# Values at rest and probabilities moving in the softmax attentions of a two-block kernel

## What is computed

```python
# first block, each of 2 layers
s = (q_nope . k_nope + q_rope . k_rope) * 96 ** -0.5      # "mla": 8 heads, width 96, values 64 wide
p = softmax(where(causal, s, neg));  o = p @ v
# top-128 of the index scores, gathered keys                # "dsa": 4 heads, one shared key and value head
p = softmax(where(valid, q . k_sel * scale, neg));  o = p @ v_sel
# second block, each of 2 layers                            # "nsa": selected and window branches,
p_s = masked_softmax(s_s, key_pos <= tq);  o_s = p_s @ v_sel   #  6 heads each in 2 groups, summed with gates
p_w = masked_softmax(s_w, m_w);            o_w = p_w @ v_win   #  12 heads in one stage
```

## Time and profile before

| | us |
|---|---|
| Runs of the kernel | 3297.77, 3294.56, 4249.05 (median 3297.77) |
| The profiled execution | 3300.15, of which the traced span is 3298.4 |
| TensorE busy in the span | 3144.2 |
| VectorE, ScalarE, GpSimd busy | 1812.1, 1302.5, 391.2 |
| mean granted TensorE clock | 0.984 of full speed |

### The profile page before, as it was taken

How to read it: one execution, slowest core, us unless ns; L and a number is a source line. 1 busy time by engine, 2 the same in 40 slices (tenths; PEclk the granted TensorE clock), 3 DMA queues, 4 the chain that set the end, 5 groups by cost and what they waited for, 6 DMA issues and landing times. The chain is left out here.

```text
span 3298.4 us, 48870 instructions
## 1 busy us (share of the span) xinstructions
PE 3144.2 (95%) x19216; PEld 2651.6 (80%) x19216; DVE 1812.1 (55%) x3220; ACT 1302.5 (39%) x2692; POOL 391.2 (12%) x374
## 2 busy tenths in 40 slices
PE   8999999999999999979999999999899999999996
PEld 6878788877878888868888878888788878788885
DVE  4875443425865424337566457474475565574744
ACT  4454432334354413233374333233443653332324
POOL 1031000001040000001213302010004034010100
PEclk9999999999999999989999999999999999999998
DMA  4111222212202222132100122222222000222230
GB/s 169 55 52 39 90 91 101 90 69 91 74 1 77 90 99 93 51 105 104 65 1 2 40 83 99 91 101 87 73 99 85 1 2 28 83 93 93 93 110 35
DMA packets 37342, 239.55 MB, mean 73 GB/s; under 512 B 4464, under 2 KB 5232, under 8 KB 15088
## 3 DMA queue, kind: packets, MB, share of 16 engines
q1 hardware_dynamic: 36528, 234.21, 20.1%
q10 hardware_dynamic: 576, 2.10, 0.2%
HBM read 234.19 MB, written 2.10 MB: 72 GB/s over the span
## 5 line engine op out<-in xcount | busy, mean ns | idle before, releaser
L265 PE MATMUL ps<-b_hl,bff_whl 128*128 128x512 f32 x704 | 274.1, 389 | 3.1 <-DVE b_hl L667 3.1
L267 PE MATMUL ps<-b_hl,bff_whl 128*128 128x512 f32 x704 | 273.9, 389 | 0.0
L266 PE MATMUL ps<-b_hl,bff_whl 128*128 128x512 f32 x704 | 273.9, 389 | 0.0
L248 DVE SCALAR_TENSOR_TENSOR bff_whl<-ring,b_cols,bff_whl 128x512 fp32r<-128x512 f32 (+1 forms) x224 | 153.2, 745 | 197.3 <-ACT bff_whl L235 197.1
L245 DVE TENSOR_TENSOR aff_whl<-ring,aff_whl 128x512 fp32r<-128x512 f32 x160 | 99.8, 685 | 222.8 <-ACT aff_whl L233 222.7
L235 ACT ACTIVATE bff_whl<-ring,b_cols 128x512 fp32r<-128x512 f32 (+1 forms) x224 | 136.6, 682 | 176.4 <-PE ps L267 176.4
L266 PE MATMUL ps<-aff_whl,a_u 128*128 128x512 f32 x512 | 204.3, 399 | 0.0
L265 PE MATMUL ps<-a_hl,aff_whl 128*128 128x512 f32 x512 | 199.5, 390 | 3.1 <-DVE a_hl L667 3.1
L265 PE MATMUL ps<-aff_whl,a_u 128*128 128x512 f32 x512 | 201.7, 394 | 0.0
L267 PE MATMUL ps<-aff_whl,a_u 128*128 128x512 f32 x512 | 200.7, 392 | 0.0
L267 PE MATMUL ps<-a_hl,aff_whl 128*128 128x512 f32 x512 | 199.2, 389 | 0.0
(11 more groups left out here) (524 smaller groups left out, 7746.5 us busy)
## 6 DMA issues: line engine op xcount, KB each, us to landing
ring<-in_a_w_ff SPq DMA_DIRECT2D x64, 1024.0 KB, 4.6
ring<-in_b_w_up SPq DMA_DIRECT2D x32, 1024.0 KB, 4.7
ring<-in_a_w_in SPq DMA_DIRECT2D x16, 1024.0 KB, 5.9
ring<-in_b_w_down SPq DMA_DIRECT2D x16, 1024.0 KB, 4.6
ring<-in_b_w_in_att SPq DMA_DIRECT2D x12, 1024.0 KB, 4.7
ring<-in_b_w_up SPq DMA_DIRECT2D x16, 768.0 KB, 4.0
ring<-in_b_w_in_conv SPq DMA_DIRECT2D x12, 768.0 KB, 4.2
ring<-in_a_w_out SPq DMA_DIRECT2D x8, 1024.0 KB, 4.8
```

Source lines behind the costliest of these rows:

```text
L248: self.c.nc.vector.scalar_tensor_tensor(out=self.part(j, 1, k), in0=src[:, k, :], scalar=g[:, row + k:row + k + 1], in1=self.part(j, 0, k) ...
L265: nc.tensor.matmul(bank, sh, mh, start=start, stop=False)
L266: nc.tensor.matmul(bank, sh, ml, start=False, stop=False)
L267: return nc.tensor.matmul(bank, sl, mh, start=False, stop=stop)
```

## The change

`softmax_attention` now takes pairs of heads (`AttentionPair`). For each head the product with the values is one group of four products after the head's fourth tile: for key tile j the values are the weights, 128 columns wide (the 64 of this head beside 64 zeros, on the side that its place in the pair says), and the turned probabilities of query tiles j to 3 move (512, 384, 256 and 128 columns). Both heads of a pair add into one PSUM bank (6), which then holds the pair's output turned: 128 value columns by 512 queries. VectorE copies it to `oT`, TensorE turns it back in four transposes to bank 7, and VectorE divides both heads at once. `pT` holds all four tiles of two heads. The turned probabilities of a head's last tile are copied by VectorE, those of the other three by ScalarE. The mask of mla goes to TensorE as in dsa and nsa. The zeros beside the values are written by GpSimd at the start of the stage (`place`); in nsa it also moves one group's values. In nsa heads h and h+3, of different groups, are a pair, and the queries are split in that order. Two copies that make float32r versions of the identity and the mask join mla's transposing stage on ScalarE.

```diff
+                    u = i - 4
+                    if ends(u):
+                        h = units[u][0]
+                        if h == 0:
+                            pe.wait_ge(placed, 1)
+                        pe.wait_ge(probsT, by_act(u))
+                        pe.wait_ge(lastT, h + 1)
+                        if h % 2 == 0 and h:
+                            pe.wait_ge(lifted, h // 2)
+                        for j in range(TT):
+                            ins = nc.tensor.matmul(c.ps[:, 6, j * P:], pairs[h // 2].values(h % 2, j),
+                                                   pT[:, h % 2, j, j * P:], start=(h % 2 == 0 and j == 0),
+                                                   stop=(h % 2 == 1 and j == last))
                         ins.then_inc(outs, 1)
+                    u = i - 6
+                    if ends_pair(u):
+                        n = units[u][0] // 2
+                        pe.wait_ge(lifted, n + 1)
+                        if n:
+                            pe.wait_ge(kept, n)
+                        for t in range(TT):
+                            ins = nc.tensor.transpose(c.ps[:, 7, t * P:(t + 1) * P], oT[:, t * P:(t + 1) * P], c.ident)
+                        ins.then_inc(returned, 1)
...
-                    u = i - 4
-                    if 0 <= u < U:
-                        h, t = units[u]
-                        pe.wait_ge(probsT, u + 1)
-                        if t == 0 and h >= 2:
-                            pe.wait_ge(kept, h - 1)
-                        for j in range(t + 1):
-                            ins = nc.tensor.matmul(c.ps[:, 6 + h % 2, t * HD:(t + 1) * HD],
-                                                   pT[:, u % 2, j * P:(j + 1) * P], heads[h].values(j),
-                                                   start=(j == 0), stop=(j == t))
...
-                        if mask is not None:
-                            s = c.ps[:, i % 4, nk - mask.shape[1]:nk]
-                            step(nc.vector.tensor_tensor(s, s, mask, ALU.add))
...
+                    u = i - 2
+                    if ends(u):
+                        h = units[u][0]
+                        dve.wait_ge(turned, u + 1)
+                        if h >= 2:
+                            dve.wait_ge(outs, h - 1)
+                        nc.vector.tensor_copy(kept_of(u), turned_of(u)).then_inc(lastT, 1)
                     u = i - 5
+                    if ends_pair(u):
+                        n = units[u][0] // 2
+                        dve.wait_ge(outs, 2 * n + 2)
+                        if n:
+                            dve.wait_ge(returned, n)
+                        nc.vector.tensor_copy(oT[:], c.banks(6)).then_inc(lifted, 1)
+                    u = i - 6
+                    if ends_pair(u):
...
+                        dve.wait_ge(probs, u + 1)
+                        step(nc.vector.reciprocal(weight[:], rsum[:, n % 2]))
+                        if pair.gate is not None:
+                            step(nc.vector.tensor_tensor(weight[:], weight[:], pair.gate, ALU.mult))
+                        dve.wait_ge(returned, n + 1)
+                        if pair.gate is None:
+                            nc.vector.tensor_tensor(pair.out, o, wide, ALU.mult).then_inc(kept, 1)
                         else:
+                            step(nc.vector.tensor_tensor(tmp[:], o, wide, ALU.mult))
+                            nc.vector.tensor_tensor(pair.out, pair.out, tmp[:], ALU.add).then_inc(kept, 1)
...
+                def rounded(act):
+                    nc.scalar.copy(ident_m[:], c.ident)
+                    nc.scalar.copy(causal_m[:], c.causal)
+                transpose_tiles(c, "mlaT", jobs, None, rounded)
+
+                def zeros_beside_values(step):
+
+                    return nc.gpsimd.memset(kv4[:, :, 1::2, 0:MLA_NOPE], 0.0)
...
+            def spread_values(step):
+                for k, v in ((B_KS, B_VS), (B_KW, B_VW)):
+                    step(nc.gpsimd.tensor_copy(proj[:, :, k + HD:k + 2 * HD], proj[:, :, v:v + HD]))
+                    ins = nc.gpsimd.memset(proj[:, :, v:v + HD], 0.0)
+                return ins
```

More of the change, by code:

```diff
@@ L2315, in rope, with __init__ @@
     step(eng.tensor_tensor(x2, x2, t1, ALU.add))
[L2318 to L2328, removed]
-    nc = c.nc
-    units = [(h, t) for h in range(len(heads)) for t in range(TT)]
-    U = len(units)
+class AttentionPair:
+    def __init__(self, scores, values, mask, out, gate=None):
+        self.scores, self.values, self.mask, self.out, self.gate = scores, values, mask, out, gate
@@ L2338, in softmax_attention @@
+def softmax_attention(c, name, pairs, place, meanwhile=None, beside=None, ready=None):
+    nc = c.nc
+    units = [(h, t) for h in range(2 * len(pairs)) for t in range(TT)]
+    U, last = len(units), TT - 1
+    by_act = lambda u: sum(t < last for _, t in units[:u + 1])
+    ends = lambda u: 0 <= u < U and units[u][1] == last
+    ends_pair = lambda u: ends(u) and units[u][0] % 2 == 1
     with ExitStack() as ctx:
         sb = lambda n, s: ctx.enter_context(nc.sbuf_tensor(name + n, s, F32))
-        p, pT = sb("p", [P, 3, SEQ]), sb("pT", [P, 2, SEQ])
@@ L2341, in softmax_attention @@
[L2341 to L2349, removed]
+        p, pT = sb("p", [P, 3, SEQ]), sb("pT", [P, 2, TT, SEQ])
@@ new lines, in softmax_attention, with _ @@
+        negmax, rsum, weight = sb("negmax", [P, 8]), sb("rsum", [P, 2, TT, 2]), sb("weight", [P, TT, 2])
+        oT, tmp = sb("oT", [P, SEQ]), sb("o", [P, TT, 2, HD])
+        wide = weight[:].unsqueeze(3).broadcast_to([P, TT, 2, HD])
+        turned_of = lambda u: c.ps[:, 4 + u % 2, 0:(units[u][1] + 1) * P].rearrange("p (j q) -> p j q", q=P)
+        kept_of = lambda u: pT[:, units[u][0] % 2, 0:units[u][1] + 1, units[u][1] * P:(units[u][1] + 1) * P]
+        with c.stage(name, "placed", "scores", "maxed", "probs", "turned", "probsT", "lastT", "outs", "lifted", "returned",
+                     "kept", "step", "pool_step", "beside_done") as (
+                block, placed, scores, maxed, probs, turned, probsT, lastT, outs, lifted, returned, kept, step_sem,
+                pool_step, beside_done):
+            @block.gpsimd
+            def _(pool):
+                step = Steps(pool, pool_step)
+                place(step).then_inc(placed, 1)
+                if meanwhile is not None:
+                    meanwhile(pool, step)
@@ L2351, in _ @@
             @block.tensor
             def _(pe):
-                for i in range(U + 4):
+                for i in range(U + 6):
                     if i < U:
@@ L2360, in _ @@
                             ready(pe, beside_done, h)
[L2361 to L2364, removed]
-                        if mask is not None:
-                            ins = nc.tensor.matmul(c.ps[:, i % 4, nk - mask[1].shape[1]:nk], mask[0], mask[1],
-                                                   start=False, stop=True)
-                        ins.then_inc(scores, 1)
+                        ident, mask = pairs[h // 2].mask(t)
+                        for n, (q, k) in enumerate(pairs[h // 2].scores(h % 2, t)):
+                            nc.tensor.matmul(c.ps[:, i % 4, 0:nk], q, k, start=(n == 0), stop=False)
+                        nc.tensor.matmul(c.ps[:, i % 4, nk - mask.shape[1]:nk], ident, mask,
+                                         start=False, stop=True).then_inc(scores, 1)
                     u = i - 2
@@ L2393, in _ @@
                 step = Steps(dve, step_sem)
-                for i in range(U + 5):
+                for i in range(U + 7):
                     if i < U:
-                        h, t = units[i]
-                        nk, mask = (t + 1) * P, heads[h].masks(t)
+                        nk = (units[i][1] + 1) * P
                         dve.wait_ge(scores, i + 1)
-                        if mask is not None:
-                            s = c.ps[:, i % 4, nk - mask.shape[1]:nk]
-                            step(nc.vector.tensor_tensor(s, s, mask, ALU.add))
                         nc.vector.tensor_reduce(negmax[:, i % 8:i % 8 + 1], c.ps[:, i % 4, 0:nk],
@@ L2421, in _ @@
             @block.scalar
             def _(act):
-                for i in range(U + 3):
+                for i in range(U + 2):
                     if i < U:
@@ L3323, in _ @@
                 wait_kept(act, 6)
-                for f in range(2):
+                for f in order[:2]:
                     query_high(f)
@@ L3327, in _ @@
                 nc.scalar.activation(flat, flat, ACT.Exp).then_inc(exps, 1)
-                for f in range(2, H):
+                for f in order[2:]:
                     query_high(f)
@@ L3857, in attentions @@
             mask_product = sb1r("identr", [P, P]), sb1r("causalr", [P, P])
-            queries = QuerySplit(nc, qT, qhl, NSA_H)
+            queries = QuerySplit(nc, qT, qhl, NSA_H, [h for n in range(NSA_R) for h in (n, n + NSA_R)])
             with ExitStack() as ctx2:
```

96 lines of the change are left out of this document (48 added, 48 removed).

## The result

The changed kernel takes 3320.67 us (median of 3 runs, 3319.76 to 3321.05) against 3297.77; the ratio is 1.0074, 95% interval 1.0045 to 1.0103. It is slower by 23 us, 5 more than the 18 of the sum, and inside the range. One of the three runs before, 4249.05, lies far off for no reason that is known; the other 53 runs of that kernel beside the experiments took 3293.5 to 3302.7. Run again beside the experiments it took 3319.31 (5 runs), ratio 1.0068 (1.0055 to 1.0082).

The account below looks back on a forecast made before the run. TensorE's queue was taken to bound nsa, with some slack in mla. Stage losses of 3.6, 2.0 and 3.4 us, twice each, add 18.0 to the 3297.77 median: 3316, own range 3303 to 3330 (70%), wider range 3290 to 3338.

Parts of the forecast that it names:

- the sum: All six stages: mla +3.6, dsa +2.0, nsa +3.4 us, twice each, 18.0 us slower.
- Value products at the same price: Values on TensorE: 2.16 us a head instead of 2.23; loads were the limit before, columns now, nearly equal.
- The first rival: Value products: wide ones are cheap, at most 0.5 ns a column, 42 us less, 3274; chance 4%.
- The return on the path: Four transposes a pair on TensorE's queue, 0.39 us, plus a stall of 0.25 waiting for VectorE's lift; none in mla.
- The masks: mla: 64 additions leave VectorE; 4 products a head join TensorE at 0.11 us each, 0.45 a head.
- The second rival: TensorE's waits absorb masks and returns, and ends cost as before: 3301 down to 3292; chance 10%.
- The centring: mla, iteration 12: VectorE's 1.47 us operation stands before the first lift; TensorE waits about 1.4 us at the return.
- The running parts: Heads between stage start and end: mla 36.8 us for six (+2.3), dsa +0.5 for two, nsa 5.14 a head.
- The stage ends: Last head's values wait for its last tile: ends 6.15 us, nsa 6.9; +1.1 mla, +1.5 dsa, +1.5 nsa.
- VectorE becomes the bound at the pair: VectorE's 2.4 us chain every second head outlasts its cover by 1 us, 24 pairs pay: 3340; chance 8%.
- The clock: Rival: pauses at the new stage ends lower the clock, six times 2 to 4 us: 3328 to 3340; chance 8%.

Follow-up runs that it names:

- 1: Kernel before with 128 instead of 64 columns moving in each value product, old form kept: 3298.38 us, ratio 1.0002.
- 2: Changed kernel with value products cut into pieces of one query tile, 10 products of 128 columns a head instead of 4: 3325.48 us, ratio 1.0082.
- 6: Two separate edits of the changed kernel: VectorE's chain of a pair spread over three tiles, 3317.92 us; return and division one tile later, 3315.78 us.
- chain spread: Changed kernel with reciprocal and gate put behind the lift (VectorE's copy to `oT`) and the addition a tile later: 3317.92 us.
- all four edits: Changed kernel with mla masks back on VectorE, last head's first three tiles multiplied early, return one tile later, VectorE's pair chain spread: 3312.59 us.

## Why the prediction held, and where its terms were off

**Value products at the same price.** Right to 0.01 us (2.15 for 2.16), and shown from both sides: the old form goes at the pace of its 20 loads and not of its columns (1), the new one takes what its columns cost at 0.85 ns, and neither width matters by more than 0.08 us a head (1, 2). The first rival, wide products that are cheap, fell: a record of 512 float32 columns takes 596 ns, and no load was saved that was not paid in columns. The sentence of the Trainium skill behind it (Perfetto Trace Analysis, Matmuls) is borne out here by no more than 0.08 us a head: the larger products took 2.15 where the smaller ones took 2.23.

**The return on the path.** Priced at 0.39 us a pair, a little low: a second one cost 0.44 to 0.46 in mla and dsa. In nsa the return and its stalls cost 0.12 us a pair more than expected (10.40 for 10.28), and the stall had two places: 0.11 to 0.12 us at the return and 0.15 at the exponential of the last tile. The prediction named the first alone, with 0.25, so the size of the stall came out by luck.

**The masks.** The term was mis-sized as an effect. Counted as 7 us of queue, they are worth 0.5 us in mla's two stages, because taking them away brings the waits back. The second rival had this right for the masks, though not for the returns. The pace of mla, 5.9 us a head, came out (11.83 a pair): the masks' work was in the sum, and the waits that it displaced were left out of it.

**The centring.** TensorE waited 1.61 us at the return at 222.32, expected 1.4; moving the return (6) gave 0.85 back, and 0.73 of waiting stayed at it.

**The running parts.** mla: 250.49 − 213.40 = 37.1 us for six heads, expected 36.8. dsa: 300.06 − 289.31 = 10.75 for two, +0.4 on the earlier trace rows, expected +0.5. nsa: 5.20 us a head, expected 5.14.

**The stage ends: the largest miss.** From the last running tile mla's end took 257.04 − 250.49 = 6.55 us and dsa's 306.61 − 300.06 = 6.55, expected 6.15; nsa's 1730.93 − 1722.83 = 8.1, expected 6.9 (1722.83 is the start of the last running value load, 1722.72, and one pace of 0.11). So the ends grew by 1.5, 1.9 and 2.8 us a layer where the sum had 1.1, 1.5 and 1.5: 4 of the 6 us that the stages lost beyond the 18. The 0.4 is spread over the steps: in mla seven transposes take 0.77 for 0.68, and VectorE's copy begins 0.3 us behind them where a step was 0.17. nsa has two waits more that the sum left out, 0.27 for the third tile's transposes and 0.63 for the last tile's. The first comes from VectorE's chain and goes with it; the second is not the chain's (6), it was 0.49 before the change, and what it was made of was not tried. The rival "VectorE becomes the bound at the pair" named the chain, whose worth is 0.13 us a pair and not 1. With nsa's running part (52.9 for 52.0) the ends make nsa +5.6 us a stage instead of +3.4, and the whole 23.8 instead of 18.0.

The forecast of 3316 against 3320.67 is near because the term that could have moved it most, the price of the values, was right; the misses, 4 us at the ends and 2 in nsa's pace, are small beside the range.

**The clock** was 1.00 in all stages of mla and dsa and 0.96 to 0.97 in nsa, before and after (with 0.50 in nsa's first 4 us both times); that rival did not happen.

## What to carry to other kernels

Before turning a product so that the wide operand moves, compare two numbers: loads × their pace, and columns × theirs. Here 20 × 0.111 and 2560 × 0.85 ns are the same 2.2 us, and all that the new layout brings besides (turning outputs back, a longer way from the last exponential to the last output) is loss. In mla, where TensorE waits for exponentials, one more tile of distance and one more buffer won 1.4 us a stage; in nsa, where it does not, the same edit cost 0.9. When the chip's scatter (some us in 3300) hides an effect, add up the stages that the edit touches: the sum of the changed kernel repeated within 0.2 us. Take the same first and last event in both kernels, and look at stages that the edit does not touch: nsa moved by up to 0.7 us a stage with the clock at its start. A wait that stands behind a long chain is not yet the chain's: shorten the chain and see whether the wait goes.

## What the runs showed of the hardware

Most of the scatter sits outside the stages and goes with the granted clock. Kernels that are the same there differ by 13 us in that rest, and the mean clock differs with it: 3013.8 us in an execution at 0.986 (chain spread), 3027.0 in one at 0.982 (all four edits).

Two executions with the same code behind nsa, windows of 10 us, of before and of the kernel with mask products alone, show one place (length; busy PE, PEld, DVE, ACT, POOL; clock):

```profile
1720.00:1730.00 10.00, 9.09 (x31) 4.98 (x32) 9.22 (x22) 7.99 (x19) 4.36 (x6) 1.00 0.00 0
1780.00:1790.00 10.00, 7.73 (x169) 7.33 (x169) 4.67 (x9) 3.90 (x12) 1.65 (x4) 0.83 0.01 2
```

```profile
1720.00:1730.00 10.00, 9.09 (x28) 5.33 (x27) 8.20 (x20) 7.04 (x17) 5.55 (x6) 0.83 0.00 0
1780.00:1790.00 10.00, 7.73 (x157) 7.33 (x158) 5.06 (x10) 3.74 (x11) 1.99 (x3) 0.83 0.01 2
```

One fall of the clock (0.83 is a part at 1.2 GHz in a window else at 2.4) is in both, the other in one only. What decides it was not tried.
